# Moving convolution taps and a loop's form around latent attention's gates in a two-block kernel

## The reference, cut to what matters

```python
h = rms_norm(h_res, pre_norm_g[i])
z = h @ w_in[i]
(pv, pg, cq, ckv, kr, mg, cu, cg, sbcx, sg, gl) = split_cols(z)
y_b = (mla_attention(...) * silu(mg)) @ w_out_mla[i]
y_c = (conformer_conv(cu, ...) * silu(cg)) @ w_out_conf[i]
gts = sigmoid(gl + gate_bias[i]).reshape(b_, l_, N_BRANCH, D_MODEL)
m = gts[:, :, 0] * y_a + gts[:, :, 1] * y_b + gts[:, :, 2] * y_c + gts[:, :, 3] * y_d

def conformer_conv(u, w_dw, b_dw, ln_g, ln_b):
    a, gate = jnp.split(u, 2, axis=-1)
    z = a * jax.nn.sigmoid(gate)
    z = causal_dwconv(z, w_dw) + b_dw      # 31 taps, 256 channels
    return jax.nn.silu(layer_norm(z, ln_g, ln_b))
```

## Time and profile before

| | us |
|---|---|
| median of three runs | 2643.38 |
| lowest and highest | 2642.81, 2646.24 |
| span of the profiled execution, first to last instruction | 2642.9 |
| PE busy in it | 2566.4 |
| DVE busy | 1473.4 |
| ACT busy | 1132.0 |
| POOL busy | 694.0 |

### The profile page before, as it was taken

How to read it: one execution, slowest core, us unless ns; L and a number is a source line. 1 busy time by engine, 2 the same in 40 slices (tenths; PEclk the granted TensorE clock), 3 DMA queues, 4 the chain that set the end, 5 groups by cost and what they waited for, 6 DMA issues and landing times. The chain is left out here.

```text
span 2642.9 us, 32352 instructions
## 1 busy us (share of the span) xinstructions
PE 2566.4 (97%) x13171; PEld 2165.7 (82%) x13171; DVE 1473.4 (56%) x1704; ACT 1132.0 (43%) x1767; POOL 694.0 (26%) x278
## 2 busy tenths in 40 slices
PE   7899999996999999999999999999999999999998
PEld 6688888885888888888888889888888788888887
DVE  3466633665547556473552676434416773839478
ACT  4355641111333323545653666333524534435354
POOL 1111112244200001422212123421331354353523
PEclk9899999998999999999999999999999999999999
DMA  3000001133365642222102113510124445361621
GB/s 136 24 25 25 25 33 48 48 127 144 136 262 199 255 175 80 96 91 79 40 33 93 53 53 111 197 48 32 34 94 158 161 162 189 109 226 48 234 85 64
DMA packets 93110, 279.74 MB, mean 106 GB/s; under 512 B 6228, under 2 KB 6612, under 8 KB 85416
## 3 DMA queue, kind: packets, MB, share of 16 engines
q1 hardware_dynamic: 88160, 253.45, 26.6%
q10 hardware_dynamic: 4808, 24.29, 2.4%
HBM read 229.27 MB, written 44.25 MB: 103 GB/s over the span
## 5 line engine op out<-in xcount | busy, mean ns | idle before, releaser
L897 POOL TENSOR_TENSOR w_lo<-w_raw,w_hi 128x1024 fp32r<-128x1024 f32 x108 | 264.4, 2450 | 1283.4 <-ACT w_hi L2144 1283.0
L1087 POOL TENSOR_TENSOR ff_wl<-ff_raw,ff_wh 128x1024 fp32r<-128x1024 f32 x86 | 259.3, 3037 | 386.1 <-ACT ff_wh L3022 386.1
L3022 ACT ACTIVATE ff_wh<-ff_raw 128x1024 fp32r<-128x1024 f32 x112 | 112.4, 1051 | 215.1 <-PE ps L2125 206.9
L2144 ACT ACTIVATE w_hi<-w_raw 128x1024 fp32r<-128x1024 f32 x108 | 113.7, 1055 | 187.7 <-PE ps L1100 79.0
L1100 PE MATMUL ps<-A_hi,w_hi 128*128 128x260 f32 (+2 forms) x680 | 163.6, 339 | 22.9 <-POOL w_lo L897 20.5
L2125 PE MATMUL ps<-A_hi,ff_wh 128*128 128x512 f32 x448 | 175.4, 392 | 2.1 <-DVE A_lo L4084 2.0
L2125 PE MATMUL ps<-A_hi,ff_wl 128*128 128x512 f32 x448 | 175.1, 391 | 0.0
L2125 PE MATMUL ps<-A_lo,ff_wh 128*128 128x512 f32 x448 | 174.9, 390 | 0.0
L2125 PE MATMUL ps<-ff_wh,A_hi 128*128 128x512 f32 x448 | 174.4, 389 | 0.1
L2125 PE MATMUL ps<-ff_wh,A_lo 128*128 128x512 f32 x448 | 174.3, 389 | 0.0
L2125 PE MATMUL ps<-ff_wl,A_hi 128*128 128x512 f32 x448 | 174.3, 389 | 0.0
(11 more groups left out here) (563 smaller groups left out, 6583.2 us busy)
## 6 DMA issues: line engine op xcount, KB each, us to landing
w_raw<-in_units SPq DMA_DIRECT2D x120, 512.0 KB, 3.2
A_hi<-token_operands SPq DMA_DIRECT2D x40, 1024.0 KB, 5.2
A_lo<-token_operands SPq DMA_DIRECT2D x40, 1024.0 KB, 7.3
ff_raw<-in_blocks SPq DMA_DIRECT2D x32, 1024.0 KB, 4.8
token_operands<-A_hi SPq DMA_DIRECT2D x10, 1024.0 KB, 10.3
token_operands<-A_lo SPq DMA_DIRECT2D x10, 1024.0 KB, 11.5
gb_raw<-in_blocks SPq DMA_DIRECT2D x10, 1024.0 KB, 9.0
X<-in_x ACTq DMA_DIRECT2D x4, 1024.0 KB, 12.3
```

What stands on the lines that cost most here:

```text
L897: nc.gpsimd.tensor_tensor(w_lo[:, slot, :], w_raw[:, slot, :], w_hi[:, slot, :].bitcast(F32), ALU.subtract).then_inc(w_lo_ready, 1)
L1087: nc.gpsimd.tensor_tensor(ff_wl[n % 2][:, 2 * e:2 * e + 2, :], src[:, 2 * e:2 * e + 2, :], ff_wh[n % 2][:, 2 * e:2 * e + 2, :].bitcast(F32 ...
L2144: fn(w_hi[:, slot, :], w_raw[:, slot, :], ACT.Copy).then_inc(w_hi_ready, 1)
L3022: fn(ff_wh[n % 2][:, 2 * e:2 * e + 2, :], src[:, 2 * e:2 * e + 2, :], ACT.Copy).then_inc(ff["wh"], 1)
```

## The change: what it does

On DVE, thirteen taps instead of seven are done ahead of the gates, and none behind the fourth pair of products: 13 + 3 x 6 = 31. The hardware loop over the two rounds is replaced by both rounds written out, with fixed addresses. The sums of tokens, which stand behind the gates, get a wait of their own on `g_mul`: for the last product in `M`. The other engines' instructions and SP's queue are as before.

```diff
-            v_taps = 7
+            v_taps = 13
...
-            def gates(b, first, kind, before_last=None):
+            def gates(b, first):
...
-                        if kind == "conv":
-                            for tap in range(6 * h, 6 * h + 6):
+                        if 2 * i + h < 3:
+                            for tap in range(v_taps + 12 * i + 6 * h, v_taps + 12 * i + 6 * h + 6):
                                 for c in range(2):
                                     chain(v.scalar_tensor_tensor(
-                                        c_acc[:, c, :], zc[:, c, ds(i * 12 + (META + v_taps + tap), S)],
-                                        vecs[:, ds(i * 12 + (VEC["conf_w"] + 31 * c + v_taps + tap), 1)],
+                                        c_acc[:, c, :], zc[:, c, META + tap:META + tap + S], vec("conf_w", 31 * c + tap),
                                         c_acc[:, c, :], ALU.mult, ALU.add))
...
-                if before_last is None:
-                    with dve.Fori(0, KT // 4) as i, chain.loop(i, KT // 4, {"conv": 24, "add": 4}[kind]):
-                        four_tiles(i)
-                else:
-                    four_tiles(0)
-                    four_tiles(1)
-
-            gates("mla", True, "conv")
+                four_tiles(0)
+                four_tiles(1)
+
+            gates("mla", True)
             dve.sem_inc(cln_f, 1)
...
             n0 = FIRST["sc_in"]
+            dve.wait_ge(g_mul, GATED["mla"] + KT + 2)
             for i in range(5):
                 token_sum(i)
```

More of the change, by code:

```diff
@@ L3415, in four_tiles @@
                     for h in range(2):
-                        if before_last is not None and i == 1 and h == 1:
-                            before_last()
                         dve.wait_ge(unit_done, i * 6 + (n0 + 3 * h + 3))
@@ L3421, in four_tiles @@
                             dve.wait_ge(g_sig, i * 4 + (GATED[b] + t + 3))
-                            m_j = M[:, ds(i * 4 + t, 1), :].rearrange("p a c -> p (a c)")
+                            m_j = M[:, i * 4 + t, :]
                             prod = pair(2 + e).rearrange("p a b -> p (a b)")
                             v.tensor_tensor(m_j, prod, sigs[e][:, :], ALU.mult).then_inc(g_mul, 1)
-                        if kind == "conv":
-                            for tap in range(6 * h, 6 * h + 6):
+                        if 2 * i + h < 3:
+                            for tap in range(v_taps + 12 * i + 6 * h, v_taps + 12 * i + 6 * h + 6):
                                 for c in range(2):
                                     chain(v.scalar_tensor_tensor(
-                                        c_acc[:, c, :], zc[:, c, ds(i * 12 + (META + v_taps + tap), S)],
-                                        vecs[:, ds(i * 12 + (VEC["conf_w"] + 31 * c + v_taps + tap), 1)],
+                                        c_acc[:, c, :], zc[:, c, META + tap:META + tap + S], vec("conf_w", 31 * c + tap),
                                         c_acc[:, c, :], ALU.mult, ALU.add))
-                if before_last is None:
-                    with dve.Fori(0, KT // 4) as i, chain.loop(i, KT // 4, {"conv": 24, "add": 4}[kind]):
-                        four_tiles(i)
-                else:
-                    four_tiles(0)
-                    four_tiles(1)
-            gates("mla", True, "conv")
+                four_tiles(0)
+                four_tiles(1)
+            gates("mla", True)
             dve.sem_inc(cln_f, 1)
```

## The result

| | before | after |
|---|---|---|
| median of four runs (before: the three above and one more), us | 2643.59 | 2630.35 |
| lowest to highest, us | 2642.81 to 2646.24 | 2628.86 to 2631.63 |
| ratio, 95% interval | | 0.9949 (0.9937 to 0.9961) |
| span of the profiled execution, us | 2642.9 | 2628.8 |

What follows compares the result with a forecast made beforehand. PE, busy 97% of 2642.9 us, bounds the kernel; its waits of 20.5 and 2.4 us follow DVE's late taps. 2642.9 - 19.8 = 2623.1, median 0.5 higher: 2623.6; range 2619.5 to 2629.5.

Steps and rivals of the forecast that it cites:

- Taps added ahead: DVE ahead of the gates: twelve more taps fit its 31.62 us idle; cost 0, at the dearest 1 to 2 us.
- a first product later than 471: Sign of a wrong forecast, at the gates: the first product was to keep its 470.5.
- The fifth rival: Gates' first products: slow added taps make products late and the kernel slower, 2653 at 6 us a tap; chance 0.02.
- first sum: DVE's first sum of tokens behind the gates: starts at 570.95, 27.75 us earlier than 598.70.
- low 0: DVE's first low part among the sums of tokens: ends at 585.6, 20.5 us earlier, not 27.75.
- low 1: DVE's next low part, whose store precedes SP's load of unit 3: ends at 592.6, 19.8 us ahead of 612.39.
- PE's wait ahead of unit 3: PE in `sc_in`, waiting for the low part `w_lo`: the wait of 20.5 us becomes 0.7.
- unit 4: PE's unit in `sc_in` that waits for `sc_u`: starts at 618.9, 19.8 us earlier, after a wait of 4.2 instead of 2.39.
- no more clock lost than before: PE's clock behind the wait for `sc_u`: the 1.7 us lost there stays as it is, change 0.
- The landing of the load: SP's load for unit 3 of `sc_in`: the piece moves whole, its high part starting 5.8 us after issue.
- The walk: DVE's sums of tokens beside POOL: each waits for the other's whole instruction; sums 3 and 4 end at 582.2.
- The third rival: DVE's sums beside POOL: no contention and the clock holds, 26.4 us gained, 2617; chance 0.09.

Runs made afterwards that it cites:

- e1: The changed kernel with DVE's first increment of `g_mul` by 2 issued ahead of the added taps, not behind them: 2622.42 us, ratio 0.9924.
- e2: The changed kernel with ten taps ahead of the gates instead of thirteen, and seven instead of six behind each of the first three pairs: 2623.69 us, ratio 0.9923.
- e4: The changed kernel with nineteen taps ahead of the gates and four behind each of the first three pairs: 2645.17 us, ratio 1.0005.
- e7: e2 with POOL making the low part of unit 2 ahead of its sums 0 and 1 instead of behind them: 2624.25 us, ratio 0.9928.
- e3: The loop written out alone, with the added wait on `g_mul`; seven taps ahead and six behind all four pairs, as before the change: 2641.95 us, ratio 0.9993.

## Why the prediction was wrong, and where it was right

**The step that failed** is "Taps added ahead". It took the 31.6 us that DVE stood idle ahead of the first product as the room for the new taps, and said that PE and ACT "wait for a product only when they write its buffers again; the first such is ACT's third sigmoid". The first such is the first sigmoid: it waits for the increment by 2 that stands for two products not yet made. The taps were moved past that increment, and an increment is no compute instruction, so it was in no row that I read. ACT wanted the increment at 448.8, 9.9 us after it came, and the low part that hangs on ACT had 4.8 more to spare, so the room was about 14.7 and not 31.6. The taps took the forecast 17.9. I gave 0 and "at the dearest some 1 to 2 us" for what measured 6.5: 3.5 of wait and 3.1 of clock. One of the forecast's own signs of being wrong, a first product later than 471, came true (476.99). e1 and e2 show it, and e4 from the other side: with the increment early, or the taps short enough, the forecast (2623.6, a ratio of 0.9925) is met: 2622.4 and 2623.7, ratios of 0.9924 and 0.9923.

**The fifth rival** had the right place, the added taps, and the wrong mechanism and threshold. It let lateness begin with the product at 470.5 (past 2.6 us a tap) and cost PE from 11 us on. ACT's lateness began at 0.83 us a tap (9.9 / 12) and PE's at about 1.2 (14.7 / 12), and the taps had 1.5. The edge at 1.2 is worked out: the runs bracket it only, with an increment at 448.9 that cost nothing (e2) and one at 456.8 that cost 3.5 of wait.

**The steps that held.** The taps end at 456.8 (forecast 456.9). The others are read with the 6.5 us taken off: first sum at 570.9 (570.95); low 0 ends at 585.7 (585.6); sum 5 starts at 589.6 (589.5); low 1 ends at 592.6 (592.6); load at 593.8 (593.75); PE's wait ahead of unit 3 0.9 (0.7); unit 4 at 619.3 (618.9), after 4.0 (4.2), and no more clock lost than before: 12.60 us at 0.86 against 12.64. The landing of the load took 0.4 us more, where the forecast had moved it whole. So 19.3 came from the sums of tokens and 6.5 went at the gates: 12.8 at unit 4, 13.2 between the medians. The spans differ by 14.1; the 1.3 more lies behind unit 4 in a single execution of each, and is not explained.

**A right number for a partly wrong reason.** The walk let sums 0 to 4 end at 582.2 by contention with POOL and had `tk_hi` 0 at 582.6 beside it, and charged the 7 us by which low 0 falls short of 27.75 to the contention. The contention was there, but e7 shows that with the five sums free of most of it low 0 starts no earlier, because `tk_hi` 0 stands behind the high part of unit 2 on ACT; only the length of low 0 (2.83 us, against 1.22 before) is POOL's. The third rival (no contention: low 1 27.8 us earlier, 2617) was thus impossible by that way; 2617 was reached by changing the queue's order.

## What to carry to other kernels

When work is put ahead of a point on an in-order engine, list every semaphore increment that it is put ahead of too, and for each one who wants it and when: the room that is safe is the gap between the increment and its first waiter (here 9.9 us), not the engine's idle time ahead of its next compute instruction (31.6). What the waiter's own results have to spare comes on top (here 4.8). An increment that stands for free buffers belongs as early as the buffers are free. And where two in-order lists (here SP's queue and ACT's list) both hold the late item ahead of the needed one, reordering one wins only until the other shows.

## What the runs showed of the hardware beyond that

How much clock a wait of PE costs is not set by its length alone. The wait of 3.5 us at the gates was followed by the low level (a granted clock of 0.50) from 462.89 to 469.03 and then by 1.00, which is the mean of 0.74 over 12.1 us (3.1 us lost). The wait of 19.3 at the same place in e4 was followed by a mean of 0.82 over 12.1 (2.2 lost); one of 4.0 ahead of unit 4 by 0.86 over 12.6 (1.8 lost), one of 2.4 before the change by 0.86 as well, and one of 0.9 by 1.00. So a wait of 3.5 us on PE can cost 6.5. Why it cost more clock than one of 19.3 stays open.

Taps written out ran closer together than in the hardware loop: 18.90 us for the twelve behind the first products, where the loop took from 472.77 to 492.89, 20.1 us, with 0.18 or 0.19 in front of each from the second on. Behind the first three pairs DVE waits for PE anyway; only behind the fourth could time come of it, and that is the 0.9 us of e3, which the times don't tell from nothing.
